# Where a gate half stands inside an attention step: between the transposes and the values, instead of at the step's end

## The chip, the core and the metric

The kernel runs on one core of one Trainium2 chip. The metric is the device time of one execution, in microseconds (us). Five instruction streams run side by side on the core and meet only at semaphores: PE (TensorE, matmuls and transposes), ACT (ScalarE), DVE (VectorE), POOL (GpSimd) and SP (SyncE, which issues the DMAs). Each stream is executed in the order in which it is written.

## What is computed

Two layers of a streaming encoder, for 512 prompt rows and for 8 streams of 16 rows each (640 rows in all, width 1024). The core of a layer of the reference:

```python
h = _rms(x, p['norm_mix'])
(fq, fk, fv, fg, bq, bk, bv, iq, ik, iw, cqa, ckva, ckpe) = jnp.split(h @ p['w_in'], ...)
# three attention branches over the same h, each: softmax(q k + bias + mask) v
ya = _over_query_blocks(fox_block, fq, qpos_b, cum[:, P:])     # 6 heads, forget gate, causal
yb = _over_query_blocks(dsa_block, bq, qpos_b, iq, iw)         # 4 heads, top-k keys of an indexer
yc = _over_query_blocks(mla_block, q_nope, q_pe, qpos_b)       # 6 heads, latent keys and values
g = jax.nn.sigmoid((h @ p['w_gate']).astype(f32)).astype(x.dtype)
ga, gb, gc = jnp.split(g, 3, axis=-1)
x = x + (ga * (ya @ p['w_fox_out']) + gb * (yb @ p['w_dsa_out']) + gc * (yc @ p['w_mla_out'])) @ p['w_o']
h2 = _rms(x, p['norm_ffn'])
gt, up = jnp.split(h2 @ p['w_ffn_in'], 2, axis=-1)
x = x + (jax.nn.silu(gt) * up) @ p['w_ffn_out']
```

What matters here is `h @ w_gate` (1024 x 3072). It needs only `h`, so its matmuls can be done at any time while the attention runs.

## The kernel before

**Stages of a layer.** Norm and transposes, the input projection, a short preparation, the **attention stage**, the output projections with the gates, `w_o`, norm, feed-forward. Every large product is split in three matmuls (high x high, high x low, low x high parts of the operands).

**The attention stage** is one loop over steps, unrolled, in every engine's stream. There are 88 items in this order: `fox` (24 items: head and tile of 128 queries, two heads of a pair one after the other), `foxs` (8 items, one a stream), `mla` (24), `mlas` (8), `dsa` (16), `dsas` (8). Steps 0 to 31 begin fox items, 32 to 63 mla items, 64 to 87 dsa items. The work of an item is spread over four steps. At step s, PE does:

- `scores(s)` into one of PSUM banks 0 to 2 (for fox and dsa pairs, both heads on the even step);
- the first half of `SIDE[s]`, small jobs beside the items (index products, keys and queries of later items). Their results go through PSUM banks 6 and 7 in turn: `bank_of(j)` (line 753) waits until ACT has emptied job j-2;
- `turn(s-2)`: transposes of the normalised probabilities (line 856), into bank 3;
- `values(s-3)`: probabilities times values, into bank 4. For pairs of tiles (line 873) only on even steps, for streams (lines 896 and 904) on every step;
- the second half of `SIDE[s]`: nothing on most steps. PE has something there on steps 22 to 29 and 54 to 60 and on 62;
- then the gate halves of `GATES_IN[s]`.

**A gate half** is `gate_half(k)` (line 709): 24 matmuls of 128 x 320 (line 720) for one of the 24 column tiles of `w_gate` and one half of the 640 rows, into bank 5. There are 48 in a layer, at most one a step, on 48 of the 88 steps. It waits for the copy that emptied bank 5 after half k-1 (`g_moved`), and on even k for the weight chunk.

**ACT at step s**, in this order: `normalise(s-1)`, `outputs(s-4)` (empties bank 4 into `at_fox`, `at_mla`, `at_dsa`), `gate_move(k)` for the halves of step **s-1** (bank 5 to `gst` or `g`, and after an odd half the copy of the next weight chunk into `w_hi`), then all moves of `SIDE[s]` out of banks 6 and 7, then `turned_out(s-2)` (bank 3 to `probs_t`), then `exp(s)`. DVE at step s: `reciprocal(s-1)` (after `exp(s-1)`), `maxima(s)` (after `scores(s)`), its part of `SIDE[s]`, and after an odd half the low part `w_lo` of the chunk. Nearly all ACT copies have line 1114, since a helper makes them; they are told apart by tile.

**Who waits for whom**: `turn(s-2)` needs `normalise(s-2)` and `turned_out(s-3)`; `values(s-3)` needs `turned_out(s-3)` and that bank 4 was emptied; `outputs(s-3)`, on ACT at step s+1, needs `values(s-3)`, and everything that ACT has at step s+1 after it stands behind it.

Of the kernel before, what the change touches and what calls it, by code (L numbers as in the profile page):

```python
# [156 lines left out]
GATES_IN = [[_k for _k in range(GATE_HALVES) if GATE_AT[_k] == _n] for _n in range(N_ITEMS + 4)]  # L157
# [43 lines left out]
def build_program(nc, io):  # L201
    ctx = ExitStack()
    with ctx:
# [154 lines left out]
        def cst(name, a=0, b=None, rows=P):  # L358
            at, w = CONST[name]
            return consts[0:rows, at + a:at + (w if b is None else b)]  # L360
# [70 lines left out]
        def item_shape(i):  # L431
            kind, h, t = ALL_ITEMS[i]
            rows = {"foxs": 96, "mlas": 96, "dsas": DH * DECT}.get(kind, P)
            blocks = t + 1 if rows == P else PAST // P + 1
            return kind, h, t, rows, blocks, blocks * P
# [5 lines left out]
        def output_parts(i):  # L441

            kind, h, t, rows, _, _ = item_shape(i)
            bank = 4
            if rows == P:
                return [(slice(0, P), h // 2, slice(t * P, (t + 1) * P), ps[:, bank, 0:P])]
            pairs = rows // 32
            cols = slice(SEQ + DECT * t, SEQ + DECT * t + DECT)

            return [(slice(HD * e, HD * e + HD), slice(0, pairs), cols,  # L450
                     stepped(ps[HD * e:HD * e + HD, bank, DECT * e:DECT * e + DECT], 2 * DECT, pairs)) for e in range(2)]
# [21 lines left out]
        def own_wait(eng, tick):  # L473

            eng.sem_inc(tick.sem, 1)
# [195 lines left out]
        def _(pe):  # L671
# [10 lines left out]
            for L in range(DEPTH):  # L682
# [28 lines left out]
                def gate_half(k):  # L711

                    m, half = divmod(k, 2)
                    if half == 0:
                        pe.wait_ge(lo_made.sem, lo_made.at(L, C_GATE + m + 1))
                    if k:
                        pe.wait_ge(g_moved.sem, g_moved.at(L, k))
                    for kk in range(KD):
                        for n, (w, x) in enumerate(w_of(m % 2)):
                            mm = pe.matmul(ps[:, 5, 0:HALF], w[:, kk * P:(kk + 1) * P], h_pair[x][:, kk, half * HALF:(half + 1) * HALF],  # L720
                                           start=kk == 0 and n == 0, stop=kk == KD - 1 and n == 2)
                    mm.then_inc((g_done, w_used)[half].sem, 1)
# [125 lines left out]
                def turn(i):  # L848
                    _, _, _, rows, blocks, _ = item_shape(i)
                    pe.wait_ge(it_norm.sem, it_norm.at(L, i + 1))  # L850
                    if i:
                        pe.wait_ge(it_pt.sem, it_pt.at(L, i))
                    if rows < 96:
                        own_wait(pe, pe_tick)
                    for j in range(blocks):
                        last = pe.transpose(ps[:, 3, j * P:j * P + rows], probs[0:rows, i % 3, j * P:(j + 1) * P],  # L856
                                            cst("ident", 0, rows, rows))
                    last.then_inc(it_tr.sem, 1)
# [169 lines left out]
                for step in range(N_ITEMS + 3):  # L1028
                    if step < N_ITEMS:
                        scores(step)  # L1030

                    half = (len(SIDE[step]) + 1) // 2
                    for kind, n in SIDE[step][:half]:
                        beside(kind, n)
                    if 2 <= step < N_ITEMS + 2:
                        turn(step - 2)
                    if step >= 3:
                        values(step - 3)
                    for kind, n in SIDE[step][half:]:
                        beside(kind, n)  # L1040
                    for k in GATES_IN[step]:
                        gate_half(k)


                pe.wait_ge(it_out.sem, it_out.at(L, N_ITEMS))
# [66 lines left out]
        def _(act):  # L1112
# [5 lines left out]
            for L in range(DEPTH):  # L1118
# [46 lines left out]
                for g, (_, width) in enumerate(GROUPS):  # L1165
                    for k in range(4):
                        c = 4 * g + k + 1
                        if c > 1:
                            hi(c, c % 2, 2 * GROUPS[c // 4][1] if c < C_GATE else 1024)
                        if c == 23:  # L1170

                            act.wait_ge(lf_abs.sem, lf_abs.at(L, 1))
                            act.activation(lf_t[:, 2], lf_t[:, 1], ACT.Exp, scale=-1.0).then_inc(lf_log.sem, 1)
                            act.wait_ge(lf_log.sem, lf_log.at(L, 1))
                            act.activation(lf_t[:, 3], lf_t[:, 2], ACT.Ln, bias=1.0).then_inc(lf_log.sem, 1)
                    for t in range(TT):
                        if t < TT - 1:
                            act.wait_ge(tile_done.sem, tile_done.at(L, 4 * g + t + 1))
                        else:
                            act.wait_ge(w_used.sem, w_used.at(L, 4 * g + 4))  # L1180
                        copy(proj[g](t), ps[:, (TT * g + t) % 8, 0:width]).then_inc(proj_out.sem, 1)
# [40 lines left out]
                def turned_out(i):  # L1222
                    _, _, _, rows, blocks, _ = item_shape(i)
                    act.wait_ge(it_tr.sem, it_tr.at(L, i + 1))
                    if i >= 4:
                        act.wait_ge(it_pv.sem, it_pv.at(L, i - 3))
                    view = lambda a: a.rearrange("p (j r) -> p j r", r=P)[:, :, 0:rows]
                    copy(view(probs_t[:, i % 4, 0:blocks * P]), view(ps[:, 3, 0:blocks * P])).then_inc(it_pt.sem, 1)
# [770 lines left out]
```

## Time and profile before

| | us |
|---|---|
| median of three runs | 2527.01 |
| lowest and highest run | 2519.61, 2527.62 |
| the profiled execution, its time | 2518.85 |
| span of its instructions | 2517.1 |
| outside the span (2518.85 - 2517.1) | 1.75 |
| PE busy in the span | 2395.5 (95%) |
| ACT busy | 961.9 (38%) |
| DVE busy | 1089.7 (43%) |
| PE busy with gate halves (line 720), of it in the first layer | 370.5, 189.4 |
| attention stage of layer 0, of layer 1 | about 480 and 460 |

PE's busy time counts overlapping matmuls once; a matmul of 128 x 320 is shown with 309 ns, but one begins every 0.15 us. The attention stage of layer 0 lies between 195 and 675 us of the span, that of layer 1 between 1460 and 1920.

### The profile page before, as it was taken

Reading aid. Unit: us, or ns where it says so; the run is one execution under the profiler, and the core shown is the slowest. Engines: PE = TensorE matmul, PEld = TensorE weight load, DVE = VectorE, ACT = ScalarE, POOL = GpSimd, SP = SyncE. Lnnn points to the kernel's source line nnn. Section 1 sums busy time; section 2 is a strip of 40 time slices with the busy share of each in tenths; the row PEclk is TensorE's granted clock in tenths of the full one; section 3 lists DMA queues with packets and bytes.
Section 4 is the critical chain, followed back from the end, with each engine's and each line's share of the span. In section 5 each row is a group of like instructions: output and inputs, shape, how many; then the busy total and the mean of one; then the engine's idle time right before and its main releaser. Section 6 shows DMA issues by size and latency. Waiting matters only on the chain.

```text
span 2517.1 us, 38757 instructions
## 1 busy us (share of the span) xinstructions
PE 2395.5 (95%) x14696; PEld 2108.2 (84%) x14696; DVE 1089.7 (43%) x2296; ACT 961.9 (38%) x1971; POOL 148.8 (6%) x116
## 2 busy tenths in 40 slices
PE   7989999999899999999999899999998999999998
PEld 7976778678797999989889676786778889899897
DVE  3557644424464332323345576454146543233232
ACT  3245654655533221111132456556456232111111
POOL 1110110110000000000012101102000000000000
PEclk9999999989899999999999999899899989999999
DMA  6222212204131222222232222231041312222222
GB/s 219 83 69 93 73 58 84 67 17 149 44 126 59 75 75 76 75 76 76 80 124 78 64 98 65 65 98 40 28 156 59 110 58 75 76 75 75 76 75 92
DMA packets 105041, 205.21 MB, mean 82 GB/s; under 512 B 37248, under 2 KB 62720, under 8 KB 104768
## 3 DMA queue, kind: packets, MB, share of 16 engines
q1 hardware_dynamic: 104896, 203.25, 24.3%
q8 instruction: 94, 1.54, 0.2%
q14 instruction: 51, 0.42, 0.1%
HBM read 176.64 MB, written 26.57 MB: 81 GB/s over the span
## 4 chain that ended last, share of the span: by engine, by line
PE 88%; DVE 4%; ACT 3%; issue 2%; DVEq 1%; POOL 1%; DMA 0%; SPq 0%; ACTq 0%; POOLq 0%
PE ps L729 29%; PE ps L702 24%; PE ps L720 14%; PE ps L904 3%; PE ps L768 2%; PE ps L856 2%; PE ps L964 2%; PE ps L873 2%; PE ps L787 1%; PE ps L813 1%; DVEq L1492 1%; PE ps L937 1%; PE ps L827 1%; PE ps L917 1%; PE ps L942 1%
## 5 line engine op out<-in xcount | busy, mean ns | idle before, releaser
L1498 DVE TENSOR_TENSOR w_lo<-raw,w_hi 128x1024 fp32r<-128x1024 f32 (+3 forms) x260 | 304.6, 1171 | 631.4 <-ACT w_hi L1114 627.7
L1114 ACT ACTIVATE w_hi<-raw 128x1024 fp32r<-128x1024 f32 (+3 forms) x260 | 263.6, 1014 | 706.6 <-PE ps L702 440.0
L729 PE MATMUL ps<-h_hi,w_hi 128*128 128x320 f32 x1664 | 382.5, 311 | 5.3 <-DVE h_lo L1507 3.9
L729 PE MATMUL ps<-h_lo,w_hi 128*128 128x320 f32 x1664 | 381.8, 311 | 0.0
L729 PE MATMUL ps<-h_hi,w_lo 128*128 128x320 f32 x1664 | 381.5, 311 | 0.0
L729 PEld LDWEIGHTS ps<-h_hi,w_hi 128*128 128x128 f32 x1664 | 281.0, 190 | 6.4 <-issue 6.1
L729 PEld LDWEIGHTS ps<-h_lo,w_hi 128*128 128x128 f32 x1664 | 280.8, 189 | 0.0
L729 PEld LDWEIGHTS ps<-h_hi,w_lo 128*128 128x128 f32 x1664 | 280.5, 189 | 0.0
L720 PE MATMUL ps<-h_hi,w_hi 128*128 128x320 f32 x768 | 254.3, 331 | 3.1 <-ACT gst L1114 1.9
L720 PE MATMUL ps<-h_lo,w_hi 128*128 128x320 f32 x768 | 244.3, 318 | 0.0
L720 PE MATMUL ps<-h_hi,w_lo 128*128 128x320 f32 x768 | 244.0, 318 | 0.0
L702 PE MATMUL ps<-w_hi,act_hi 128*128 128x512 f32 x440 | 173.4, 394 | 0.0
L702 PE MATMUL ps<-w_lo,act_hi 128*128 128x512 f32 x440 | 172.5, 392 | 0.0
L702 PE MATMUL ps<-w_hi,act_lo 128*128 128x512 f32 x440 | 170.8, 388 | 0.0
L720 PEld LDWEIGHTS ps<-h_hi,w_hi 128*128 128x128 f32 x768 | 151.8, 198 | 13.2 <-issue 9.0
L702 PE MATMUL ps<-w_hi,h_hi 128*128 128x384 f32 (+3 forms) x480 | 161.2, 336 | 0.3 <-DVE w_lo L1498 0.3
L702 PE MATMUL ps<-w_lo,h_hi 128*128 128x384 f32 (+3 forms) x480 | 160.2, 334 | 0.0
L702 PE MATMUL ps<-w_hi,h_lo 128*128 128x384 f32 (+3 forms) x480 | 159.9, 333 | 0.0
L1475 POOL TENSOR_TENSOR rsq<-ssq,mhalf 128x12 f32<-128x12 f32 (+3 forms) x56 | 118.9, 2123 | 584.1 <-DVE ssq L1531 498.8
L720 PEld LDWEIGHTS ps<-h_lo,w_hi 128*128 128x128 f32 x768 | 151.4, 197 | 0.0
L720 PEld LDWEIGHTS ps<-h_hi,w_lo 128*128 128x128 f32 x768 | 150.6, 196 | 0.0
L1114 ACT ACTIVATE probs<-probs,mx 128x256 f32<-128x256 f32 (+5 forms) x176 | 101.6, 577 | 100.7 <-DVE mx L1695 100.7
(303 smaller groups left out, 3611.4 us busy)
## 6 DMA issues: line engine op xcount, KB each, us to landing
raw<-in_weights SPq DMA_DIRECT2D x212, 512.0 KB, 3.5
gates<-gst SPq DMA_DIRECT2D x72, 160.0 KB, 1.8
g<-gates SPq DMA_DIRECT2D x12, 960.0 KB, 5.4
raw<-in_weights SPq DMA_DIRECT2D x24, 384.0 KB, 3.0
out_y_prompt<-x_sb SPq DMA_DIRECT2D x12, 512.0 KB, 4.6
kc<-in_cache_fox_k SPq DMA_DIRECT2D x16, 384.0 KB, 3.3
vc<-in_cache_fox_v SPq DMA_DIRECT2D x16, 384.0 KB, 3.6
x_sb<-out_y_prompt SPq DMA_DIRECT2D x8, 512.0 KB, 4.4
```

The lines of the kernel that those rows point to most:

```text
L702: mm = pe.matmul(ps[:, (bank0 + t) % 8, 0:width], x_pair[x][:, k0 + kk, t * P:(t + 1) * P], w[:, kk * width:(kk + 1) * width], start=first ...
L720: mm = pe.matmul(ps[:, 5, 0:HALF], w[:, kk * P:(kk + 1) * P], h_pair[x][:, kk, half * HALF:(half + 1) * HALF], start=kk == 0 and n == 0, s ...
L729: mm = pe.matmul(ps[:, 2 * pair + half, 0:HALF], w[:, (w0 + kk) * P:(w0 + kk + 1) * P], x_pair[x][:, kk, half * HALF:(half + 1) * HALF], s ...
L768: last = pe.transpose(ps[0:cols, bank, n * P:n * P + rows], src, cst("ident", 0, rows, rows))
L787: mm = pe.matmul(ps[:, (i + e) % 3, 0:width], q[r, t * P:(t + 1) * P], k[r, 0:width], start=True, stop=not masked)
L856: last = pe.transpose(ps[:, 3, j * P:j * P + rows], probs[0:rows, i % 3, j * P:(j + 1) * P], cst("ident", 0, rows, rows))
L873: mm = pe.matmul(ps[HD * e:HD * e + HD, bank, 0:P], v, probs_t[:, (i - 1 + e) % 4, j * P:(j + 1) * P], start=j == 0, stop=j == blocks - 1)
L904: mm = pe.matmul(ps[:, bank, 32 * pair:32 * pair + 32], v, pt[:, j * P + 32 * pair:j * P + 32 * pair + 32], start=j == 0, stop=j == blocks ...
L964: pe.matmul(ps[:, bank, 0:384].rearrange("p (h d) -> p h d", h=MH), ctb[:, n % 6, m, :], wkv[:, :, part:part + HD], start=True, stop=True) ...
L1114: return act.activation(dst, src, ACT.Copy, scale=scale)
L1475: pool.tensor_tensor(rsq[:, n % RSLOT, 0:width], ssq[:, n % RSLOT, 0:width], mhalf[:, 0:width], ALU.pow).then_inc(sq_root.sem, 1)
L1498: dve.tensor_tensor(w_lo[slot][:, 0:width], raw[slot][:, 0:width], w_hi[slot][:, 0:width].bitcast(F32), ALU.subtract).then_inc(lo_made.sem, 1)
```

## The change

In PE's stream alone, the gate halves of a step are issued after `turn(s-2)` and before `values(s-3)`. Before, they were the last thing of the step, after the values and after the second half of the side jobs. The streams of ACT, DVE, POOL and SP are the same, row for row.

```diff
                     if 2 <= step < N_ITEMS + 2:
                         turn(step - 2)
+                    for k in GATES_IN[step]:
+                        gate_half(k)
                     if step >= 3:
                         values(step - 3)
                     for kind, n in SIDE[step][half:]:
                         beside(kind, n)
-                    for k in GATES_IN[step]:
-                        gate_half(k)
```

Of the 48 gate halves of a layer, 18 stand on odd steps among pairs of tiles where neither values nor a second half of side jobs comes after the transposes; there the two orders are the same. The other 30 move.

PE at steps 22 and 23 of layer 0, before. L856 are transposes, L873 values, L917 an index product, L720 the gate half (24 rows, the first and the last stand), L768 with `p_m` a job of step 23, L923 the first job of stream 1's keys:

```order
L856 MATMUL ps<-consts,probs 128x128 x3
L873 MATMUL ps<-probs_t,p_v 64x128 x4
L917 MATMUL ps<-xt_156 128x256
L720 MATMUL ps<-h_hi,w_hi_57 128x320
...
L720 MATMUL ps<-h_hi,w_lo_59 128x320
L768 MATMUL ps<-consts,p_m 128x128 x3
L856 MATMUL ps<-consts,probs 128x128 x3
L923 MATMUL ps<-consts,lfc_125 6x128
```

The same place now:

```order
L856 MATMUL ps<-consts,probs 128x128 x3
L720 MATMUL ps<-h_hi,w_hi_57 128x320
...
L720 MATMUL ps<-h_hi,w_lo_59 128x320
L873 MATMUL ps<-probs_t,p_v 64x128 x4
L917 MATMUL ps<-xt_156 128x256
L768 MATMUL ps<-consts,p_m 128x128 x3
L856 MATMUL ps<-consts,probs 128x128 x3
L720 MATMUL ps<-h_hi,w_hi_57 128x320
```

The first half has gone ahead of the values and of the index product. The second one, of step 23, has gone ahead of the jobs of stream 1's keys, so that it follows its own step's transposes at once.

PE at steps 59 and 60 of layer 0, before. L904 are values of a stream, L964 products that make keys or values of a stream, L768 with `ckvc` transposes of a latent, L827 the next step's scores:

```order
L856 MATMUL ps<-consts,probs 128x96 x3
L904 MATMUL ps<-probs_t,v_mlas 128x32 x2
...
L964 MATMUL ps<-wkv,ctb 128x384 x2
L768 MATMUL ps<-consts,ckvc_144 128x128 x2
L720 MATMUL ps<-h_hi,w_hi_58 128x320
...
L720 MATMUL ps<-h_hi,w_lo_60 128x320
L827 MATMUL ps<-ktbm,qzm 32x256 x3
```

And now:

```order
L856 MATMUL ps<-consts,probs 128x96 x3
L720 MATMUL ps<-h_hi,w_hi_58 128x320
...
L720 MATMUL ps<-h_hi,w_lo_60 128x320
L904 MATMUL ps<-probs_t,v_mlas 128x32 x2
...
L964 MATMUL ps<-wkv,ctb 128x384 x2
L768 MATMUL ps<-consts,ckvc_144 128x128 x2
L827 MATMUL ps<-ktbm,qzm 32x256 x3
```

The values and both side jobs now stand between the gate half and the next scores.

## Rows read from the trace of the kernel before

**Rows 1.** The page: span of the profiled execution

```profile
span 2517.1 us, 38757 instructions
```

**Rows 2.** Attention stages by windows: length, busy time of each engine, PE clock, DMA

```profile
195.00:675.00 480.00, 450.69 (x2997) 358.85 (x2998) 231.99 (x633) 270.98 (x713) 36.46 (x16) 0.94 0.23 76
1460.00:1920.00 460.00, 434.05 (x2906) 347.66 (x2905) 219.45 (x601) 262.03 (x687) 36.48 (x16) 0.94 0.23 75
```

**Rows 3.** Waits of PE, 195 to 675: in total, times, longest

```profile
PE ps L856 <- ACT probs_t L1114: 5.1, 5, 2.1
PE ps L896 <- ACT at_dsa L1114: 4.9, 3, 3.3
PE ps L768 <- issue: 4.5, 6, 2.0
```

**Rows 4.** Timeline of PE, step 3: start, length, what, idle time before it

```profile
205.20 0.30 PE L856 MATMUL ps<-consts,probs 128*128 128x128 f32 x1 [2.10 <-ACT probs_t L1114]
```

**Rows 5.** The chain that ended last: the gate half of step 22

```profile
286.06 3.72 PE ps L720 x24
```

**Rows 6.** Timeline of PE, steps 23 and 24

```profile
289.95 0.49 PE L856 MATMUL ps<-consts,probs 128*128 128x128 f32 x3
290.37 0.38 PE L923 MATMUL ps<-consts,lfc 128*6 128x128 f32 x2
...
295.60 0.63 PE L827 MATMUL ps<-ktb,qz 128*32 128x256 f32 x6
```

**Rows 7.** Timeline of ACT, steps 22 to 24

```profile
286.16 0.38 ACT L1258 ACTIVATE relu<-ps 128x256 f32<-128x256 f32 x1 [1.30 <-PE ps L917]
286.44 0.48 ACT L1114 ACTIVATE probs_t<-ps 128x384 f32<-128x384 f32 x1
286.81 0.69 ACT L1219 ACTIVATE probs<-ps,mx 128x512 f32<-128x512 f32 x1
...
288.45 0.26 ACT L1114 ACTIVATE at_fox<-ps 128x128 f32<-128x128 f32 x1
289.82 0.44 ACT L1114 ACTIVATE gst<-ps 128x320 f32<-128x320 f32 x1 [1.11 <-PE ps L720]
...
298.60 0.41 ACT L1114 ACTIVATE qa<-ps 128x288 f32<-128x288 f32 x1 [1.51 <-PE ps L937]
```

**Rows 8.** Timeline of PE, step 59: the last side job

```profile
512.47 0.41 PE L768 MATMUL ps<-consts,ckvc 128*128 128x128 f32 x2 [0.42 <-issue]
```

**Rows 9.** Timeline of ACT, steps 59 and 60

```profile
513.00 0.41 ACT L1114 ACTIVATE ctb<-ps 128x256 f32<-128x256 f32 x1
...
515.05 0.41 ACT L1114 ACTIVATE at_mla<-ps 64x48 f32<-64x48 f32 x2
516.43 0.44 ACT L1114 ACTIVATE gst<-ps 128x320 f32<-128x320 f32 x1 [0.97 <-PE ps L720]
516.76 1.05 ACT L1114 ACTIVATE w_hi<-raw 128x1024 fp32r<-128x1024 f32 x1
518.91 0.49 ACT L1114 ACTIVATE v_mlas<-ps 128x384 f32<-128x384 f32 x1 [1.10 <-PE ps L964]
```

**Rows 10.** Timeline of PE: first jobs waiting in steps 29 and 30

```profile
356.93 0.83 PE L768 MATMUL ps<-consts,ka 128*96 128x128 f32 x6 [0.95 <-ACT qt L1114]
...
368.08 0.38 PE L768 MATMUL ps<-consts,qa_new 128*32 128x128 f32 x2 [0.33 <-ACT qn_mla L1114]
```

**Rows 11.** Timeline of PE, steps 54 and 55

```profile
467.51 0.41 PE L768 MATMUL ps<-consts,ckvc 128*128 128x128 f32 x2 [0.79 <-issue]
...
473.78 1.56 PE L964 MATMUL ps<-wkv,ctb 128*128 128x384 f32 x4 [0.55 <-ACT rope_past L1114]
```

**Rows 12.** A slow stretch of PE by windows (length, busy times, clock, DMA)

```profile
374.33:384.57 10.24, 10.24 (x48) 10.18 (x48) 2.29 (x8) 2.73 (x11) 0.00 (x0) 0.50 0.28 87
```

**Rows 13.** Timeline of PE, layer 0: steps 67 and 87

```profile
577.26 0.41 PE L720 MATMUL ps<-h_hi,w_hi 128*128 128x320 f32 x1 [0.42 <-ACT gst L1114]
...
660.24 0.63 PE L896 MATMUL ps<-probs_t,bvrep 128*128 128x64 f32 x4 [0.42 <-ACT at_dsa L1114]
```

## The prediction

> **What bounds the kernel now.** I read the page first, then the attention stages by windows, then PE's waits there, and last the timelines of PE and ACT step by step. The span is 2517.1 us [rows 1]. The change touches the two attention stages alone, and there PE is busy for 450.69 of 480 and 434.05 of 460 us, while ACT is busy for a little over half [rows 2]. So PE's stream sets the time, and all that can move it is PE's idle time: 29.3 us in the first stage (480 - 450.69), 26.0 in the second. The reader is to see in PE's waits that these are many small ones, nearly all of them for a copy that ACT had not made yet: `turned_out` (5.1 us), the emptying of bank 4 (4.9), the two banks of the side jobs (4.5, "issue" there) [rows 3]. The gate halves are what PE does while ACT catches up. The question is therefore what each half covers at its old place, and what it covers at the new one.
>
> **What the change removes and adds.** No instruction is added or taken away, and the order of ACT, DVE, POOL and SP is unchanged. PE has the same matmuls. One half at the full clock is 3.72 us [rows 5]; I use 3.7. Of the 48 halves of a layer 18 do not move. For the other 30 I go by what now stands behind the half instead of ahead of it.
>
> (a) Values alone behind it: 22 of the 30. `turn(s-2)`, half, `values(s-3)` is the same PE work as before, in another order. The copy of bank 3 is made under the half; before, it was made under values and half. Nothing waits there. What is new is on ACT: `outputs(s-3)` now stands ready only when the values end, and `gate_move` is queued behind it. It costs where the next step has a half too, which needs bank 5 empty. At step 67 this already costs 0.42 us [rows 13]. The copy into `at_fox` takes 0.26 us for a pair, the one into `at_mla` 0.41 for a stream [rows 7, 9]. Some 7 halves a layer have a neighbour like that; at 0.15 us (half of the copy is behind PE's transposes, the copy of the half itself no longer trails the half) they cost 1.1 us. At step 87 the half now covers a wait for bank 4, 0.42 us [rows 13], and the same copy costs some 0.3 at the end of the stage. Sum of (a): about 1.0 us a layer, bounds 0 (all behind other work) and 30 x 0.4 = 12 (the copy exposed each time).
>
> (b) Side jobs behind it: steps 22, 23, 26, 29, 54, 56, 59, 62. This carries the forecast. ACT moves **all** side jobs of step s before it does `turned_out(s-2)` and `exp(s)`. These jobs now come out of PE 3.7 us later, so the chain that follows starts 3.7 us later, while PE reaches step s+1 when it always did. Take steps 59 and 60. The last side job is the latent [rows 8], its copy `ctb` began at 513.00 and would begin at 516.7. From there to `at_mla` ACT and DVE took 515.05 - 513.00 = 2.05 us (`probs_t`, exp, reciprocal, normalise), which gives 518.75; then two output copies, 0.4; `gst`, 516.76 - 516.43 = 0.33; `w_hi`, about 1.0 [rows 9]. ACT is at the first side job of step 60 at 520.5. Before, it began that copy at 518.91, when PE had made the job [rows 9], and PE's next job but one waits for it. ACT is late by 1.6; I take 1.5. Before, the half hid this whole chain; now ACT sits idle under the half and PE waits after it. Step 29 is the same with an odd half: PE waited 0.33 us there for a bank, and the stage's own step without a half, the one before, has 0.95 in that place [rows 10]; with `gst` and `w_hi` added (0.33 + 1.0) on 0.95, and 0.33 taken off, 1.95; I take 1.7. At step 54, also odd, the wait of 0.79 for a bank ahead of the latent goes, since the half stands there now, and the wait of 0.55 after it grows [rows 11]; with longer rows of probabilities the chain is about 2.0, so 2.0 - 0.8 = 1.2. Steps 26, 56 and 62 have even halves, without `w_hi`: 1.5 - 1.0 = 0.5 at most, I take 0.5, 0.2 and 0.2.
>
> Steps 22 and 23 are the dearest place. The second index product's copy (`relu`) goes from 286.16 to 289.86, `probs_t` begins 0.28 later and takes 0.48 [rows 7], so the transposes of step 23 begin at 290.7 instead of 289.95 [rows 6]. Right behind them stands the half of step 23, which needs bank 5. ACT gets to that copy after exp, reciprocal, normalise and `at_fox`: 288.45 + 3.7 = 292.15, and with 0.2 and 0.44 [rows 7] bank 5 is empty at 292.8. Without any wait the half could begin at 290.37, where the next job began [rows 6]. PE is 2.5 late. Then stream 1's keys stand behind this half too: the scores of step 24 come at 295.60 + 2.5 = 298.1 [rows 6], but ACT ends its chain (some 1.7 us of key copies from 296.6, 2.3 as from `relu` to `at_fox`, 0.33, 1.0) at about 302.0, where `qa` would be due at 298.60 + 2.5 = 301.1 [rows 7]. Another 0.9. Together 3.4.
>
> Sum of (b): 3.4 + 0.5 + 1.7 + 1.2 + 0.2 + 1.5 + 0.2 = 8.7 us a layer. Both layers run the same program, so the change costs 2 x (8.7 + 1.0) = 19 us. On the profiled execution (2518.85, that is the span and 1.75 around it) this gives 2538; on the median of the runs, 2527.01, which is 8 us above the profiled one, 2546.
>
> **A rule weighed.** Row 205.20 shows transposes that waited 2.10 us for the copy of bank 3, which the transposes before them had filled [rows 4]. The Trainium skill, Perfetto Trace Analysis, section Matmuls under Optimizing Tensor Performance, says that independent matmul groups should rotate through PSUM banks, so that emptying one overlaps the next group. By it a half (bank 5) right behind transposes (bank 3) and ahead of values (bank 4) is the better order, and this change would gain; by the rows the half overlapped the same copy before, with the values between.
>
> **Rivals.**
>
> *The waits behind a half go (faster).* If the half right behind the transposes gave ACT time to be ahead for the whole next step, half of the 14.5 us in the three rows of waits would go, 7 us a layer: 2527 - 14 = 2513. It decides if ACT, once ahead, stays ahead. For it: 0.79 and 0.42 us do vanish at steps 54 and 87 [rows 11, 13]. Against it: the longest wait for bank 3 stands in step 3, which has the same order in both [rows 4], and ACT can't get ahead, since it is held by copies of jobs that PE makes later. The rule above would give this result.
>
> *The lateness is absorbed (no change that can be measured).* If the later stalls of PE in the same stretch (0.95 at 356.93, those at 54 and 55) start from something other than ACT's chain, they take up the delay, and less than half of (b) is left: 2 x 3.5 = 7, 2534 or less. Against it: the stalls name ACT tiles of the same chain [rows 10, 11].
>
> *The clock, or every output copy (more).* In one stretch of 10.24 us PE ran at a granted clock of 0.50, its 1.2 GHz level; ahead of it PE had made small matmuls for streams, with no half since step 29 [rows 12]. The mean of each stage is 0.94 [rows 2]. The keys of steps 29 and 62 now stand behind their halves, so the runs of small matmuls until the next half are 1 to 2 us longer. If two more such stretches come in each layer, at some 4 us each (10.24 us at half speed, part of it idle anyway), that is 16 us: 2562. The same page of the Trainium skill, Matmul Optimizations, says that the engine scales with utilisation and wants matmuls back to back in batches, which would speak for this rival. If the output copy is exposed at every half of (a), the upper bound there, the time is 2568.
>
> **How the numbers follow.** Forecast 0.60, at 2546, with its own range 2532 to 2562; absorbed 0.20, 2521 to 2534; more 0.14, 2562 to 2580; faster 0.06, 2505 to 2519. A measurement of this kernel can tell about 0.3%, 7.6 us, from no change. Slower by more than that: 0.58 of the forecast and the 0.14, 0.72. Within: 0.22. Faster: 0.06. The range leaves out the faster case and the upper part of "more", and reaches into the absorbed one: 2524 to 2564. The runs before differ by 8 us among themselves, which is in it.
>
> **What would show it.** In the profile after: PE's idle time in the two stages up by about 19 us; a wait of some 2 us of the half of step 23 for ACT's `gst`, in both layers, at line 720; PE's waits at side jobs for ACT tiles (`qt`, `qn_mla`, `rope_past`, `v_mlas`) longer after steps 29, 54 and 59 and nearly unchanged after 26, 56 and 62; ACT's wait for line 720 ahead of `gst` and `g` gone on most of the 30 steps, and in its place a wait for values. If PE's idle time is unchanged, the absorbed case holds; if it fell at bank 3 and bank 4, the faster one; if busy time rose with the mean clock below 0.94, the clock one. I am wrong if ACT is found ahead of PE at the first side jobs of steps 24, 30, 55 and 60.

## The result: slower, by 0.46% and in a second comparison by 0.67%

| | before | after |
|---|---|---|
| median, us | 2524.68 | 2534.36 |
| lowest and highest | 2517.64, 2527.62 | 2525.94, 2550.12 |
| runs | 14 | 14 |
| profiled execution | 2518.85 | 2543.98 |

The ratio is 1.0046, with a 95% interval of 1.0030 to 1.0062. The difference of the medians is 9.7 us, that of the means 11.6. A second comparison, run with the experiments, gave 2540.14 (4 runs) against 2523.32 (13 runs): 1.0067, interval 1.0050 to 1.0084, 16.8 us. The forecast was 2546, 19 us more than before, with a range of 2524 to 2564.

The two profiled executions stand 25 us apart, more than the medians. The one of before was among its fastest runs, the one of after the second slowest of its 14. So the profiles are used for where time goes, and the medians for how much.

**PE's busy and idle time.** The page's span, and its row of busy time for PE (the first number), of the changed kernel:

```profile
span 2542.2 us, 38757 instructions
PE 2397.7 (94%) x14696; PEld 2108.1 (83%) x14696; DVE 1090.2 (43%) x2296; ACT 959.0 (38%) x1971; POOL 148.8 (6%) x116
```

Before, PE was busy for 2395.5 us of 2517.1 [rows 1]. Busy time rose by 2.2 us; idle time rose from 121.6 to 144.5, by 22.9. The same by windows, cut exactly from the first to the last transposes of each attention stage. The columns are window, length, busy time of PE, PEld, DVE, ACT and POOL, the granted clock and the DMA's share and GB/s. The kernel before:

```profile
202.80:666.40 463.60, 439.37 (x2935) 350.36 (x2934) 221.46 (x618) 262.27 (x696) 36.46 (x16) 0.94 0.23 75
1448.40:1908.90 460.50, 436.55 (x2936) 348.34 (x2934) 221.31 (x618) 262.25 (x696) 36.48 (x16) 0.95 0.23 76
```

The changed kernel:

```profile
204.90:678.10 473.20, 439.44 (x2935) 349.01 (x2934) 221.47 (x618) 260.97 (x696) 36.47 (x16) 0.95 0.23 73
1463.30:1933.60 470.30, 436.51 (x2936) 347.49 (x2935) 220.30 (x614) 260.29 (x694) 36.47 (x16) 0.95 0.23 73
```

PE is busy for the same time in both (439.37 and 439.44, 436.55 and 436.51). Its idle time goes from 24.2 to 33.8 us in the first stage and from 24.0 to 33.8 in the second: 19.4 us in the two, where 2 x 9.7 had been forecast. The other 3.5 us of idle time lie outside the stages, where the two kernels have the same order on every engine; this was not followed up.

**Which waits.** PE's waits from 195 to 690 us of the changed kernel (total, times, longest), to hold against [rows 3]:

```profile
PE ps L856 <- ACT probs_t L1114: 5.7, 6, 2.1
PE ps L964 <- ACT rope_past L1114: 5.4, 3, 2.6
PE ps L896 <- ACT at_dsa L1114: 4.7, 3, 3.3
PE ps L768 <- issue: 4.4, 7, 1.3
PE ps L720 <- ACT gst L1114: 3.6, 5, 1.5
...
PE ps L768 <- ACT qn_mla L1114: 2.0, 1, 2.0
...
PE ps L827 <- ACT rope_past L1114: 1.0, 1, 1.0
```

Bank 3, bank 4 and "issue" are where they were (5.1, 4.9 and 4.5 before). What grew are the halves' waits for bank 5, the jobs that wait for `qn_mla` (0.3 us before), and the waits of line 964 for `rope_past` (3.0 before). New is a wait of scores, line 827, for `rope_past`. On the page, the first product of the halves has the idle time ahead of it in its last column. Before it was 3.1 us, 1.9 of them for `gst`. After:

```profile
L720 PE MATMUL ps<-h_hi,w_hi 128*128 128x320 f32 x768 | 254.4, 331 | 9.2 <-ACT gst L1114 7.6
```

**Steps 22 and 23, the dearest place.** Timeline of PE in the changed kernel. The half of step 22 runs between the rows 289.94 and 293.94:

```profile
289.94 0.55 PE L856 MATMUL ps<-consts,probs 128*128 128x128 f32 x3
...
293.94 0.66 PE L873 MATMUL ps<-probs_t,p_v 128*64 128x128 f32 x8
294.53 0.69 PE L917 MATMUL ps<-xt 32*128 32x256 f32 x2
295.15 0.55 PE L768 MATMUL ps<-consts,p_m 128*128 128x128 f32 x3
296.23 0.52 PE L856 MATMUL ps<-consts,probs 128*128 128x128 f32 x3 [0.53 <-ACT probs_t L1114]
298.25 0.41 PE L720 MATMUL ps<-h_hi,w_hi 128*128 128x320 f32 x1 [1.50 <-ACT gst L1114]
```

And ACT at the same place:

```profile
290.11 0.38 ACT L1258 ACTIVATE relu<-ps 128x256 f32<-128x256 f32 x1 [0.35 <-PE ps L917]
295.32 0.38 ACT L1258 ACTIVATE relu<-ps 128x256 f32<-128x256 f32 x1 [4.83 <-PE ps L917]
295.60 0.48 ACT L1114 ACTIVATE probs_t<-ps 128x384 f32<-128x384 f32 x1
...
296.98 0.72 ACT L1114 ACTIVATE probs<-probs,mx 128x512 f32<-128x512 f32 x1 [0.23 <-DVE mx L1695]
297.61 0.26 ACT L1114 ACTIVATE at_fox<-ps 128x128 f32<-128x128 f32 x1
297.77 0.43 ACT L1114 ACTIVATE gst<-ps 128x320 f32<-128x320 f32 x1
```

For 4.83 us ACT has nothing it may do: the next copy in its stream is that of the second index product, which PE makes only after half and values. Before, that wait was 1.30 us [rows 7]. The transposes that could be copied lie in bank 3 all the while. As soon as the product is there ACT is late, and PE waits 0.53 us for the next transposes and 1.50 for bank 5.

**Steps 30, 55, 60 and 63.** Timeline of PE, changed kernel: the first waits after the halves of steps 29, 54, 59 and 62. The last row is of scores, the others of side jobs:

```profile
380.39 0.38 PE L768 MATMUL ps<-consts,qa_new 128*32 128x128 f32 x2 [2.00 <-ACT qn_mla L1114]
...
491.21 1.56 PE L964 MATMUL ps<-wkv,ctb 128*128 128x384 f32 x4 [2.62 <-ACT rope_past L1114]
...
536.04 0.52 PE L768 MATMUL ps<-consts,k_mlas 128*128 128x128 f32 x3 [1.33 <-issue]
...
562.16 1.08 PE L827 MATMUL ps<-ktbm,qzm 128*32 128x256 f32 x6 [1.03 <-ACT rope_past L1114]
```

The first was 0.33 [rows 10], the second 0.55 [rows 11]; the third and the fourth are new. The fourth is of another kind: the scores of step 63 need the keys of the stream that step 62's last side job has just made, and the half no longer stands between the two while ACT copies them. The second layer has the same wait, also 1.03.

### The profile page after: what moved, and what is told of

Same layout as the page of the kernel before. It is cut to its first block, busy times and chain, and to the rows that moved or that the text cites. A ratio compares the mean times of both kernels' runs of the same rounds, so it can differ in the third digit from the quotient of the medians.

```text
span 2542.2 us, 38757 instructions
## 1 busy us (share of the span) xinstructions
PE 2397.7 (94%) x14696; PEld 2108.1 (83%) x14696; DVE 1090.2 (43%) x2296; ACT 959.0 (38%) x1971; POOL 148.8 (6%) x116
## 4 chain that ended last, share of the span: by engine, by line
PE 86%; ACT 4%; DVE 4%; issue 2%; DVEq 1%; POOL 1%; DMA 0%; SPq 0%; ACTq 0%; POOLq 0%
PE ps L729 29%; PE ps L702 24%; PE ps L720 14%; PE ps L904 3%; PE ps L768 2%; PE ps L856 2%; PE ps L964 2%; PE ps L873 2%; PE ps L787 1%; PE ps L813 1%; DVEq L1492 1%; PE ps L917 1%; PE ps L690 1%; PE ps L937 1%; PE ps L942 1%
## 5 line engine op out<-in xcount | busy, mean ns | idle before, releaser
L720 PE MATMUL ps<-h_hi,w_hi 128*128 128x320 f32 x768 | 254.4, 331 | 9.2 <-ACT gst L1114 7.6
L720 PE MATMUL ps<-h_lo,w_hi 128*128 128x320 f32 x768 | 245.1, 319 | 0.0
L720 PE MATMUL ps<-h_hi,w_lo 128*128 128x320 f32 x768 | 244.6, 319 | 0.0
L720 PEld LDWEIGHTS ps<-h_hi,w_hi 128*128 128x128 f32 x768 | 152.5, 199 | 14.9 <-ACT gst L1114 7.3
L720 PEld LDWEIGHTS ps<-h_lo,w_hi 128*128 128x128 f32 x768 | 152.0, 198 | 0.0
L720 PEld LDWEIGHTS ps<-h_hi,w_lo 128*128 128x128 f32 x768 | 151.3, 197 | 0.0
```

## The experiments

Each kernel is the changed one or the kernel before with the edit shown. "Idle" is PE's idle time in the two stages together (48.2 us before, 67.6 after), from the profile of each kernel. **Time at the lower clock** is 2 x span x (1 - mean granted clock): the clock has two levels, 1.0 and 0.5 of full speed, so this is how long PE had the lower one. It is averaged over all runs of a kernel, since it varies from run to run, and set against that of the kernel before in the same comparison (171.5, 175.8, 176.3 and 176.5 us in the four). Single runs of the kernel before lie up to 50 us from one another in it, so with 10 to 12 runs a difference of 5 to 8 us is not clear of noise.

### Part (a) and part (b) apart

The new place on all steps but the eight with side jobs behind it:

```diff
+                    early = step not in (22, 23, 26, 29, 54, 56, 59, 62)
-                    for k in GATES_IN[step]:
+                    for k in GATES_IN[step] if early else ():
                         gate_half(k)
                     ...
+                    for k in () if early else GATES_IN[step]:
+                        gate_half(k)
```

> The new order on all steps except 22, 23, 26, 29, 54, 56, 59 and 62, where side jobs stand behind the values; there the gate half stays at the step's end. 22 halves of a layer move. Theory 1 (idle time, and the clock gives some back): PE's idle time in both attention stages together rises by about 2 us against the kernel before (the copy of the outputs ahead of the copy of the half), not by 19; the time is 2 us above the kernel before or less, since the clock's part may show here too. Rival (the loss comes from the values behind the halves, by the copy of the outputs): most of the 9.7 us stays, +8 us or more.

Measured: 2516.46 against 2521.83, ratio 0.9983 (0.9971 to 0.9994). Idle +2.1 us, as summed for (a). But the kernel is not 2 us slower than before, it is 5.4 us faster, with 14.4 us less at the lower clock (157.1).

The new place on the eight steps alone (`early = step in (...)`, the same list):

> The complement: only the halves of steps 22, 23, 26, 29, 54, 56, 59 and 62 stand ahead of the values and side jobs; all others stay at the step's end. Theory 1: the whole loss of idle time, 2 x 8.7 = 17 us, is here, and the time is 8 to 17 us above the kernel before, as the clock gives some of it back or not; the wait of the half of step 23 for ACT's copy of bank 5 is in it. Rival (the values behind the halves): at most +3 us.

Measured: 2540.97, ratio 1.0075 (1.0055 to 1.0094), 19.1 us more, above the 8 to 17 expected. Idle +14.6 for the 17 expected, and 0.6 us less at the lower clock: here the clock gave nothing back. So (b) carries the whole loss, and more than the whole change loses.

The dearest two of them alone (`early = step in (22, 23)`):

> Only the halves of steps 22 and 23 move. The prediction put 3.4 us a layer here: 0.7 at the transposes of step 23, 1.8 at the half of step 23, which waits for bank 5, and 0.9 at the first products of step 24. Idle time +6 to 7 us for both layers, time +5 to +8 us. Rival (a delay here is taken up by later stalls of PE, which are not tied to ACT): idle time of the stage +1 us a layer or less, time within 2 us.

Measured: 2529.39 against 2522.87, ratio 1.0029 (1.0016 to 1.0041), 6.5 us. Idle +5.8 (2 x 2.9, for the 2 x 3.4 forecast), and the timeline of PE has the same two waits as the changed kernel, 0.53 and 1.50:

```profile
294.85 0.52 PE L856 MATMUL ps<-consts,probs 128*128 128x128 f32 x3 [0.53 <-ACT probs_t L1117]
296.87 0.42 PE L720 MATMUL ps<-h_hi,w_hi 128*128 128x320 f32 x1 [1.50 <-ACT gst L1117]
```

### Is it ACT's order?

If the whole loss comes from `turned_out` and `exp` standing behind copies of jobs that PE has not made yet, it must go when they stand ahead of them. In the changed kernel, in ACT's stream:

```diff
-                    for kind, n in SIDE[step]:
+                    cut = (len(SIDE[step]) + 1) // 2
+                    for kind, n in SIDE[step][:cut]:
                         beside(kind, n)
                     if 2 <= step < N_ITEMS + 2:
                         turned_out(step - 2)
                     if step < N_ITEMS:
                         exp(step)
+                    for kind, n in SIDE[step][cut:]:
+                        beside(kind, n)
```

> The changed kernel with one edit on ACT: it does turned_out(s-2) and exp(s) between the first and the second half of the step's side moves, so that this chain no longer waits for side jobs that PE makes behind the gate half. Theory 1: the waits of PE after steps 22, 23, 29, 54 and 59 go for the most part; 12 to 17 us of idle time less than the changed kernel, which is 2 to 8 us below the kernel before. Rival (PE's late arrival at the values and side jobs themselves is what costs, not ACT's order): no gain on the changed kernel, +8 to +10 us on the kernel before.

Measured: 2521.09 against 2521.83, ratio 1.0000 (0.9986 to 1.0013). Idle 57.3 us, 10.2 less than in the changed kernel, where 12 to 17 were expected; the time is level with the kernel before, not 2 to 8 us below it. ACT at step 22 there:

```profile
289.01 0.38 ACT L1258 ACTIVATE relu<-ps 128x256 f32<-128x256 f32 x1 [0.34 <-PE ps L917]
289.42 0.49 ACT L1114 ACTIVATE probs_t<-ps 128x384 f32<-128x384 f32 x1
289.81 0.68 ACT L1219 ACTIVATE probs<-ps,mx 128x512 f32<-128x512 f32 x1
...
294.21 0.39 ACT L1258 ACTIVATE relu<-ps 128x256 f32<-128x256 f32 x1 [3.62 <-PE ps L917]
```

And PE at step 23:

```profile
294.42 0.49 PE L856 MATMUL ps<-consts,probs 128*128 128x128 f32 x3
295.75 0.41 PE L720 MATMUL ps<-h_hi,w_hi 128*128 128x320 f32 x1 [0.83 <-ACT gst L1114]
```

The wait of 0.53 at the transposes is gone, that of the half down from 1.50 to 0.83. The waits after steps 29 and 54 fell too, from 2.00 to 0.80 and from 2.62 to 1.38. Those after steps 59 and 62 stayed at 1.33 and 1.03. So `turned_out` and `exp` standing behind the late jobs make about half of the loss of idle time, 10.2 of 19.4 us. The rest lies in the copies of the late jobs themselves: after step 59, ACT took 5.26 us from its first copy of a late job to that of the next step's (`v_mlas`) with the edit and without it, and after step 62 the scores wait for such a copy directly. The time of this kernel owes something to the clock as well, with 20.7 us less at the lower one. The same edit on the kernel before, to see what it is worth by itself:

> Control of e3_act_first: the kernel before, with the same edit on ACT (turned_out(s-2) and exp(s) between the two halves of the step's side moves). The theory: with the gate half at the step's end the chain is covered anyway where there is a half, so the edit gives at most 1 to 2 us of idle time, from the few steps with side jobs and no half; the time is within 3 us of the kernel before. Rival (the edit is a gain of its own, and e3_act_first took back its loss by that): 8 us or more below the kernel before.

Measured: 2522.20 against 2522.87, ratio 0.9991 (0.9978 to 1.0004), idle +0.9. Nothing that shows by itself: what it saves in the changed kernel is idle time that the change had made.

### The clock

The kernel with (a) alone gained where only a loss had been summed. Three kernels looked for the place. First the halves of steps 62 and 66, after which the kernel before had a stretch at the lower clock:

> Only the halves of steps 62 and 66 move ahead of the values. In idle time this should cost next to nothing (0 to 0.5 us a layer). Theory 1's second part (the new places break up long runs of small stream matmuls, so that less of them runs at the lower clock, which gives back what the median lacks against the 19 us): 2 to 4 us a layer less, 4 to 8 us below the kernel before, and a higher mean clock. Rival (the clock is unmoved on the mean of runs): within 1 us of the kernel before.

Measured: 2521.47 against 2521.83, ratio 0.9991 (0.9978 to 1.0003), idle +2.3, 4.9 us less at the lower clock. The expected 4 to 8 us did not come, and no gain shows.

Then the steps where values of streams stand behind the half (`early = step in (32, 34, 64, 66, 85, 87)`):

> Only the halves of steps 32, 34, 64, 66, 85 and 87 move ahead of the values: those whose values are of streams (matmuls of 32 or 64 columns), without side jobs behind them. The theory for e1_sides_old's gain (5.4 us less with 2 us more of idle time, 157 us at the lower clock instead of 171): the halves now break up the runs of stream values where the clock fell, so this kernel alone has most of it: some 160 us at the lower clock, idle time +0.5 us, 3 to 6 us below the kernel before. Rival (the gain lies with the halves among pairs of tiles, or is chance): within 1.5 us of the kernel before.

Measured: 2516.03 against 2522.87, ratio 0.9967 (0.9956 to 0.9978). Idle +1.5, time at the lower clock 149.4, 26.4 less. Six halves a layer, moved from behind the small matmuls of a stream to ahead of them, give back 6.8 us net, more than the 3 to 6 expected. That is also more clock time than the 14.4 us of the kernel with all 22 halves of (a) moved, these six among them.

Last the changed kernel itself once more, for its clock beside the kernel before in the same comparison:

> The changed kernel itself, beside the kernel before on one chip, so that both have their granted clocks from the same place and time. Theory (the change costs 19.4 us of idle time and gives some of it back through fewer microseconds at the lower clock): the median is 9 to 12 us above the kernel before, and the time at the lower clock, 2 x span x (1 - mean clock) averaged over the runs, is 10 to 16 us less than that of the kernel before (about 161 against 171 to 176). Rival (the difference of 11 to 15 us between the clocks was one between chips or days, and the missing 8 to 10 us went elsewhere): the time at the lower clock is within 4 us of the kernel before's.

Measured: 2540.14 against 2523.32. That is 16.8 us, where 9 to 12 were expected. Time at the lower clock 167.6 against 176.5, 8.9 less, short of the 10 to 16 expected; with 4 and 13 runs it is uncertain by some 8 us, so it does not rule out the rival's 4. In the first comparison the changed kernel had 160.7. All 18 runs of the changed kernel together have 162.2, all 93 of the kernel before in the experiments 174.7. So the change gives back some us through the clock. The 6.9 us between 160.7 and 167.6 are worth about 3.5 us, half of what separates 9.7 from 16.8; the other half is not explained.

### A better order

If side jobs behind a half cost idle time and halves ahead of a stream's values save clock, the order should be: transposes, second half of the side jobs, half, values. On every step, against the changed kernel:

```diff
                         turn(step - 2)
+                    for kind, n in SIDE[step][half:]:
+                        beside(kind, n)
                     for k in GATES_IN[step]:
                         gate_half(k)
                     if step >= 3:
                         values(step - 3)
-                    for kind, n in SIDE[step][half:]:
-                        beside(kind, n)
```

> A version that might beat both: on every step the second half of the side jobs comes right after the transposes, then the gate half, then the values. The side jobs are again ahead of the half, so ACT's chain is covered, and the values are behind it as in the changed kernel. The theory: idle time of both stages +2 us against the kernel before, as in e1_sides_old, fewer us at the lower clock (155 or so against 171), time 4 to 9 us below the kernel before. Rival (values themselves must be early, since ACT's outputs and then the copy of bank 5 stand behind them at steps with much side work): +5 us or more.

Measured: 2499.36 (2497.27 to 2503.17) against 2522.87, ratio 0.9913 (0.9897 to 0.9929). This beats the kernel before by 23.5 us. The changed one, in its two comparisons, had medians 35 and 41 us above it. Its stages by windows:

```profile
205.70:656.70 451.00, 428.06 (x2935) 340.01 (x2933) 220.47 (x614) 261.63 (x694) 36.46 (x16) 0.97 0.23 76
1440.20:1889.10 448.90, 425.03 (x2935) 337.67 (x2934) 221.54 (x618) 262.59 (x696) 36.46 (x16) 0.98 0.24 78
```

Its page's row of busy time:

```profile
PE 2374.6 (95%) x14696; PEld 2088.8 (84%) x14696; DVE 1090.4 (44%) x2296; ACT 962.1 (39%) x1971; POOL 148.8 (6%) x116
```

Idle time is that of before (22.9 and 23.9). What fell is the busy time, from 439.37 to 428.06 and from 436.55 to 425.03, with the same instructions, while the clock rose from 0.94 and 0.95 to 0.97 and 0.98. I had expected 4 to 9 us; the clock gave the rest. With the side jobs ahead, the waits of 0.53 and 1.50 us at step 23, of 1.33 after step 59 and of 1.03 after step 62 are gone, and the one after step 29 is 0.33 again. So this kernel, more than ACT's edit, shows what the loss of idle time came from: side jobs behind a half.

Most of the gain lies between the transposes of step 60 and those of step 68. The same work of the first layer by windows, in the kernel before and with the best order:

```profile
520.65:581.60 60.95, 58.51 (x351) 49.50 (x350) 9.90 (x28) 25.02 (x78) 3.17 (x1) 0.80 0.08 26
523.61:573.56 49.95, 49.02 (x352) 41.59 (x350) 9.98 (x28) 25.12 (x78) 3.17 (x1) 0.97 0.09 32
```

That is 11.0 us less, 9.5 of it busy time (58.51 and 49.02) at a clock of 0.97 in place of 0.80. The second layer has 60.92 and 48.39 us in this place, another 12.5. A smaller place is the end of the fox streams. A stretch of PE at clock 0.50 there, by windows, in the changed kernel (in the kernel before it is 10.24 us [rows 12]):

```profile
380.96:398.03 17.07, 17.07 (x83) 15.45 (x83) 3.57 (x12) 5.88 (x19) 0.00 (x0) 0.50 0.25 78
```

The same stretch with the best order:

```profile
376.38:383.21 6.83, 6.83 (x31) 6.77 (x31) 2.47 (x9) 2.56 (x9) 0.00 (x0) 0.50 0.31 97
```

In the changed kernel PE had waited 2.00 us just ahead of the stretch (the row 380.39 above). With the best order that wait, in PE's timeline, is as long as before [rows 10]:

```profile
370.38 0.38 PE L768 MATMUL ps<-consts,qa_new 128*32 128x128 f32 x2 [0.33 <-ACT qn_mla L1114]
```

To find which steps matter, the order was put on three of the eight alone, `early = step in (56, 59, 62)`, and on the other five, `(22, 23, 26, 29, 54)`, the rest as before:

> The kernel before, with the order side jobs, gate half, values on steps 56, 59 and 62 alone (e6_sides_gate_values has it on every step). In the profile of e6_sides_gate_values 16 of its 24 us showed up between the transposes of steps 60 and 67, where the kernel before ran at the lower clock. If the place of the halves of the steps around 60 does that by itself, this kernel has idle time as before (+1 us), 15 to 25 us less at the lower clock and is 7 to 12 us below the kernel before. Rival (the gain there needs the halves of steps 64 and 66 too, and those of 32 and 34 at the other place): 3 us or less below.

Measured: 2514.10 against 2523.05, ratio 0.9963 (0.9947 to 0.9979), idle +0.3, 28.6 us less at the lower clock.

> The kernel before with the order transposes, second half of the side jobs, gate half, values on steps 22, 23, 26, 29 and 54 alone, the counterpart of the kernel that had this order on steps 56, 59 and 62 (8.9 us below before). The kernel with it on all steps was 23.5 us below, the one with it on all steps but these eight 5.4 below (there the order was transposes, half, values). Theory (each place shortens its own runs of small matmuls, and the parts add): 23.5 - 5.4 - 8.9 = 9 us below the kernel before, 6 to 12, with 12 to 20 us less at the lower clock and PE idle 23 to 25 us a stage. Rival (a stretch at the lower clock that is broken at one place comes back at the next unless all places are changed): 0 to 4 us below.

Measured: 2523.40 against 2523.32, ratio 0.9998 (0.9982 to 1.0015), idle +0.3, 7.6 us less at the lower clock. The expected 9 us did not come; the time is about that of the rival, 0 to 4 us below. Its windows show the second stage no better than before:

```profile
203.80:660.90 457.10, 432.37 (x2935) 343.95 (x2934) 221.42 (x618) 262.28 (x696) 36.47 (x16) 0.96 0.24 76
1446.10:1908.50 462.40, 438.61 (x2936) 350.05 (x2935) 220.18 (x614) 261.98 (x694) 36.47 (x16) 0.95 0.23 74
```

Three kernels shown here have the halves of the best order, each in some of its places: this one, the one on 56, 59 and 62, and the one with the new place on all but the eight steps. They give -0.1 + 9.0 + 5.4 = 14.3 us, the best one 23.5. This alone does not show that the places do not add, since the best order does one thing more that none of the three does. On steps 24, 27, 28, 58 and 60, which have no half, it puts the second half of the side jobs ahead of the values. PE at step 24 there; in the kernel before, line 873 comes straight after line 856:

```profile
304.46 0.60 PE L856 MATMUL ps<-consts,probs 128*128 128x128 f32 x4
...
305.74 1.03 PE L768 MATMUL ps<-consts,kc 128*128 128x128 f32 x6
306.70 0.88 PE L873 MATMUL ps<-probs_t,p_v 128*64 128x128 f32 x12
```

What this is worth by itself was not run.

Last, ACT's edit from above on the best order:

> e6_sides_gate_values with the edit on ACT of e3_act_first. With the side jobs ahead of the half the ACT chain is covered already, so the edit has nothing left to save but what steps without a half lose: 0 to 2 us less idle time, within 3 us of e6_sides_gate_values, that is 20 to 26 us below the kernel before. Rival (ACT's order still holds PE up after the side jobs at steps 29 and 59): 4 us or more below e6_sides_gate_values.

Measured: 2512.57 against 2523.05, ratio 0.9959 (0.9947 to 0.9971), 13 us worse than without it, where a difference within 3 us had been expected. Idle 53.4 us, 6.6 more. With this PE order the second half of the side jobs is ready early, and ACT now makes PE wait for it. Two rows of PE there; the kernel without the edit has no wait at these jobs:

```profile
309.25 0.41 PE L768 MATMUL ps<-consts,kc 128*128 128x128 f32 x2 [0.25 <-ACT gate_past L1114]
...
329.22 0.85 PE L768 MATMUL ps<-consts,kc 128*128 128x128 f32 x6 [0.50 <-ACT ct L1114]
```

### All of them in one account

"Whole idle" is the page's span less PE's busy time, against the 121.6 us of before. The sum adds half of the change in time at the lower clock to it, since PE does half as much in such a microsecond.

| kernel | whole idle | lower clock | sum | means differ by |
|---|---|---|---|---|
| changed, second comparison | +21.9 | -8.9 | +17.5 | +17.8 |
| all but the eight steps | +3.8 | -14.4 | -3.4 | -5.3 |
| the eight steps alone | +18.1 | -0.6 | +17.8 | +19.3 |
| 22 and 23 alone | +5.8 | +3.7 | +7.7 | +6.3 |
| changed, ACT's edit | +11.7 | -20.7 | +1.4 | +1.0 |
| before, ACT's edit | +0.3 | -5.8 | -2.6 | -2.1 |
| 62 and 66 alone | +2.1 | -4.9 | -0.4 | -1.3 |
| streams' steps | +4.5 | -26.4 | -8.7 | -8.0 |
| best order, 56, 59, 62 | +3.2 | -28.6 | -11.1 | -10.1 |
| best order, 22 to 54 | +2.9 | -7.6 | -0.9 | -1.1 |
| best order | +0.8 | -44.2 | -21.3 | -23.0 |
| best order, ACT's edit | +8.3 | -36.9 | -10.2 | -10.1 |

The sum stands within 2 us of the measured difference in all twelve. Idle time and clock leave nothing of size for a third term. This is an account of where the time went; why the clock moved it does not say. For the first comparison of the changed kernel the clock of the runs before is not listed; with 171.5 to 176.5 us, as in the others, its sum is 22.9 - 5.4 = 17.5 down to 22.9 - 7.9 = 15.0, against 11.6 measured. These 3 to 6 us stay unexplained.

## Why the prediction was right, and where it was off

The time fell in the range, and the kernel is slower by more than 0.3%, the case that had 0.72. The range was wide, and by its time alone the first result, 2534.36, could as well be that of the absorbed rival (2534 or less): it is the idle time in the stages that tells the two apart. The difference, 9.7 us and then 16.8, was forecast as 19. Of the 11.6 us between 2546 and 2534.36, 2.3 are the median of before, 2527.01 then and 2524.68 with more runs.

| step of the working | forecast, us a layer | measured, us a layer |
|---|---|---|
| (a) values alone behind the half | 1.0 | 1.0 (that part alone) |
| transposes and half of step 23, of it | 2.5 | 2.0 (0.53 + 1.50) |
| the same with the products of step 24 | 3.4 | 3.2 (second layer), 2.9 alone |
| 26 | 0.5 | 0.3 |
| 29 | 1.7 | 1.7 (2.00 less 0.33) |
| 54 | 1.2 | 1.25 |
| 56 | 0.2 | 0.4 |
| 59 | 1.5 | 1.1 |
| 62 | 0.2 | 1.0 (1.03, in both layers) |
| (b) all eight | 8.7 | 7.3 alone |
| both together | 9.7 | 9.5 and 9.8 |

The figures for 24, 26, 54, 56 and 59 are how much the start of the transposes of the next steps, set against the same transposes of before, falls further behind from one step to the next. A stretch at the lower clock lies at steps 23 and 24 of the first layer, so the second layer is taken there. The single terms add up to 9.0 for the 8.7 forecast, in part by luck: 56 and 62 cost 1.0 more than forecast, the others 0.8 less. Step 62 is a term that was sized wrong. It was taken from ACT's chain without the weight copy, 1.5 - 1.0 = 0.5 at most, and the waits after 62 were to stay nearly unchanged; what it costs is the scores' wait for the copied keys, which the sum did not have.

- **The mechanism held.** ACT moves all side jobs of a step before `turned_out` and `exp`; jobs that come 3.7 us later from PE make this chain late, and nothing covers it. This was the step that carried the forecast, and moving those two ahead on ACT took half of it away; putting the side jobs ahead of the half took all of it away. In the chain worked out for step 59 the two were not what counted: the wait there stayed at 1.33 with them ahead. Its sign in the profile held as well: ACT's waits for line 720 fell from 78 of 144.5 us together to 22 of 29.6.
- **The bounds.** (a) was between 0 and 12 us a layer, and the value taken, 1.0, was measured as 1.0. The upper bound counted all 30 halves; the 22 of (a) give 22 x 0.4 = 8.8 us, and 2562 in place of 2568. The copy into bank 4's tile is exposed only where the next half has to wait for bank 5: at step 67 the wait grew from 0.42 [rows 13] to 0.83. Alone the parts make 2.1 + 14.6 = 16.7 us; together 19.4. That a late ACT is worse for a neighbouring half would explain it, but is not shown.
- **The step that failed is the last one of the sum**, "2 x (8.7 + 1.0) = 19 us. On the profiled execution (...) this gives 2538". It carried idle time over to device time one to one, and so took the clock as unchanged. The clock was thought of only as a rival, with the opposite sign: two more stretches at the lower clock in each layer, 2562. In the runs of the second comparison the change had 8.9 us less of it, which gives back 4.5. The reasoning was that the runs of small matmuls get longer behind a half on steps 29 and 62. That did happen in one place, 10.24 to 17.07 us at the end of the fox streams, after a new wait of 2.00 us. But the halves that moved ahead of values alone had the opposite effect: 14.4 us less with (a) alone, 26.4 less with the six halves ahead of streams' values. The half now stands between a stream's transposes and its values, and the values run on into the next scores; that the clock follows from this is a guess that no run tests.
- **The rivals.** "The waits behind a half go" fell: bank 3 and bank 4 have 5.7 and 4.7 us of waits, for 5.1 and 4.9. "Absorbed" fell too: the two stages have 9.5 and 9.8 us more idle time, as much as was forecast without absorption. The rule of the Trainium skill (Perfetto Trace Analysis, Matmuls), that independent groups should rotate through banks so that emptying one overlaps the next group, was in the prediction a reason for a gain. The trace does not bear it out for this change: the half in bank 5 stands right behind the transposes in bank 3, yet ACT's copy of bank 3 began at 295.60, after the half, because ACT was held by another bank's job.
- **No row of the profile of before tells how much the clock gives back.** What could have stood in the working is that the term has two signs: a block that moves leaves small matmuls together in one place and parts them in another.

**What stays open.** Why the clock falls where it does. The same order gives 28.6 us less on three steps and 7.6 on five others, and whether the gains of the parts add is open, since the best order also moves side jobs on five steps without a half. The experiments name places, not a rule. Not settled either is whether the changed kernel's 160.7 us at the lower clock in one comparison and 167.6 in the other are more than chance, and what the rest of the idle time after steps 59 and 62 would need on ACT.

## What to carry to other kernels

A large block of work that one engine does is cover for the engine that empties its results: before moving it, look at what the emptying engine has next in its own fixed order, and keep ahead of the block whatever that engine needs first. Here it is enough to put the side jobs ahead of the half, and a loss of 10 to 17 us becomes a gain of 23. Where an engine's clock changes with what it does, sum idle time and time at the lower clock apart, and read the second from many runs; a reordering that saves next to no idle time can still be worth close to 1%.

## What the runs showed of the hardware

- **The clock moves a tuned kernel by close to 1% with no instruction changed.** The same 14696 matmuls kept PE busy for 2395.5 us in one order and for 2374.6 in another, with mean granted clocks of 0.966 and 0.975 in these two profiles, and 175.8 and 131.6 us at the lower clock on the mean of the runs. It was low while PE had work without a gap, too: in the rows above PE was busy for 17.07 of 17.07 us at a clock of 0.50. The Trainium skill (Perfetto Trace Analysis, Matmul Optimizations) says that the matmul engine scales its power with utilisation and wants matmuls back to back in batches. By these runs it is also a question of where the batches stand: the halves kept their 24 matmuls, and PE's idle time in the stages was nearly the same (48.2 and 46.8 us).
- **Most of the spread between runs of one kernel is the clock too.** Over 93 runs of the kernel before, from 2513.4 to 2528.9 us, the mean clock went from 0.971 to 0.962, and time and time at the lower clock have a correlation of 0.92. The slope within one kernel is 0.29 us for each us at the lower clock, less than the 0.5 that fits between kernels; why is not known.
- **One profile can mislead by this much.** The two first profiles differ by 25 us, the means by 11.6. In both, the stages had the same 51.2 and 44.4 us at the lower clock, so they alone would have said that the clock plays no part.
